# Three residual buffers, the next expert's copies ahead of the hidden product, filler products on TensorE, another group order, and the last x2 tile stored from ScalarE's queue

## What is computed

```python
x = x + token_mixer(rmsnorm(x), ...)          # its last product: merged @ w_out
x = x + hier_moe(rmsnorm(x), ...)
# hier_moe: 4 groups of 8 experts; top 1 group, then top 2 experts in it
lg = xt @ w_rg + b_rg; g_sel = top_k(softmax(lg), 1)
le = (xt @ w_re + b_re)[g_sel]; e_sel = top_k(softmax(le), 2)
h = silu(xb @ w1[e]) * (xb @ w3[e]);  y = (h @ w2[e]) * gate
```

## Time and profile before

| | us |
|---|---|
| median of 3 runs | 1255.5 |
| lowest, highest | 1253.0, 1255.56 |
| the profiled execution: its time | 1254.98 |
| its span, first to last instruction | 1253.3 |
| TensorE busy | 1114.9 (89% of the span) |
| VectorE, ScalarE, GpSimd busy | 510.9, 421.9, 229.9 |
| mean granted TensorE clock | 0.945 of full speed |
| read from and written to memory | 278.57 MB and 39.06 MB |

### The profile page before, as it was taken

The page is one execution under the profiler, slowest core; times in us unless marked ns, Lnnn a source line. Parts: engine busy times, 40 slices in busy tenths (PEclk is TensorE's granted clock), DMA queues, the critical chain, the costliest instruction groups (busy, mean ns, idle before and its releaser), DMA issues.

```text
span 1253.3 us, 15692 instructions
## 1 busy us (share of the span) xinstructions
PE 1114.9 (89%) x5136; PEld 684.8 (55%) x5136; DVE 510.9 (41%) x837; ACT 421.9 (34%) x658; POOL 229.9 (18%) x275
## 2 busy tenths in 40 slices
PE   5899999999988977999995699999999999898960
PEld 4688888888855645788784233333333333333320
DVE  5511111113237746755346244343515453424128
ACT  5322222223145655533114133333333342424222
POOL 0111101110007001000000033333323332423220
PEclk9899999999998967999996799999999999999985
DMA  8633331711160001746548989999999999999816
GB/s 320 233 118 118 112 114 50 284 47 45 50 252 2 1 1 42 246 133 241 195 158 331 420 340 375 419 420 419 421 419 365 421 420 420 420 420 420 336 36 276
DMA packets 69248, 308.89 MB, mean 246 GB/s; under 512 B 9025, under 2 KB 9153, under 8 KB 43873
## 3 DMA queue, kind: packets, MB, share of 16 engines
q1 hardware_dynamic: 56144, 273.86, 55.1%
q0 software_dynamic: 13072, 34.63, 7.2%
HBM read 278.57 MB, written 39.06 MB: 253 GB/s over the span
## 4 chain that ended last, share of the span: by engine, by line
PE 57%; DMA 22%; DVE 8%; ACT 6%; issue 5%; SPq 1%; DVEq 1%; ACTq 0%; POOLq 0%; POOL 0%
DMA rawe<-in_w 17%; PE ps L569 11%; PE ps L571 11%; PE ps L570 11%; PE ps L843 11%; PE ps L870 3%; ACT cur L1168 3%; PE ps L651 1%; DMA xres<-in_x_prompt 1%; PE ps L672 1%; PE ps L833 1%; DMA xrow<-in_x_sample 1%; DVE att L1316 1%; PE ps L684 1%; ACT prob L984 1%
## 5 line engine op out<-in xcount | busy, mean ns | idle before, releaser
L569 PE MATMUL ps<-whi,xTh 128*128 128x512 f32 x480 | 188.9, 394 | 18.5 <-DVE wlo L1199 14.0
L570 PE MATMUL ps<-wlo,xTh 128*128 128x512 f32 x480 | 188.5, 393 | 0.0
L571 PE MATMUL ps<-whi,xTl 128*128 128x512 f32 x480 | 188.2, 392 | 0.0
L843 PE MATMUL ps<-cur13a,xT 128*64 128x512 f32 x656 | 156.5, 619 | 25.9 <-DVEq L1601 25.1
L1199 DVE TENSOR_TENSOR wlo<-raw,whi 128x2048 fp32r<-128x2048 f32 x27 | 61.7, 2291 | 216.3 <-ACT whi L893 216.3
L843 PE MATMUL ps<-cur13b,xT 128*64 128x512 f32 x656 | 148.6, 592 | 0.0
L870 PE MATMUL ps<-cur,hT 128*64 128x512 f32 x640 | 146.2, 598 | 0.0
L1576 DVE COPY xT<-ps 128x512 f32<-128x512 f32 x41 | 28.3, 691 | 288.9 <-PE ps L833 288.9
L932 ACT ACTIVATE zst<-ps,rstd 128x512 f32<-128x512 f32 x60 | 41.3, 689 | 234.9 <-PE ps L571 232.8
L1168 ACT ACTIVATE cur<-rawe 128x4096 f32 x31 | 112.2, 3620 | 2.9 <-issue 0.2
L569 PEld LDWEIGHTS ps<-whi,xTh 128*128 128x128 f32 x480 | 91.1, 190 | 38.0 <-issue 18.8
(11 more groups left out here) (219 smaller groups left out, 1429.8 us busy)
## 6 DMA issues: line engine op xcount, KB each, us to landing
rawe<-in_w SPq DMA_DIRECT2D x96, 2048.0 KB
raw<-in_w_in SPq DMA_DIRECT2D x20, 1024.0 KB, 5.9
z_scratch<-zst POOLq DMA_DIRECT2D x60, 256.0 KB, 2.3
gat<-z_scratch SPq DMA_DIRECT2D x12, 512.0 KB, 3.7
xn_scratch<-rrow POOLq DMA_DIRECT2D x6, 1024.0 KB, 4.6
ya<-y_scratch SPq DMA_DIRECT2D x6, 1024.0 KB, 9.9
raw<-in_w_out SPq DMA_DIRECT2D x4, 1024.0 KB, 7.6
xcol<-in_x_cols SPq DMA_DIRECT2D x6, 512.0 KB, 10.2
```

The source lines that it names most:

```text
L569: pe.matmul(out, ah, bh, start=first, stop=False)
L570: pe.matmul(out, ah, bl, start=False, stop=False)
L571: return pe.matmul(out, al, bh, start=False, stop=last)
L843: mm = pe.matmul(ps[0][u * CAP:(u + 1) * CAP, :], xT[:, c, h * CAP:(h + 1) * CAP], cur13[h][:, :, c * 512 + u * 256:c * 512 + u * 256 + 25 ...
```

## The change

It joins six edits. (1) `xres` becomes three buffers with a semaphore each; the first three loads are queued ahead of expert 0, the others as soon as a buffer is free. (2) The store of the last x2 tile moves from SyncE to ScalarE, ahead of its squaring; SyncE queues expert 1 once the last w_out product is done and no longer after the last addition. (3) In `next_up` the copies of the next expert's w1 and w3 stand ahead of `xT` and `hh`; `cur13a` is released by a new semaphore at the middle of `up(b)`. (4) TensorE issues six products of 128x512 into `ps[7]`, which nothing reads, ahead of its wait for the number of blocks. (5) The groups are taken in the order 2, 0, 1, 3. (6) Router columns and ranks are laid out to match, on the host and in the constants.

```diff
+ORDER = (2, 0, 1, 3)
-    put("grank", NG - np.arange(NG))
+    put("grank", NG - np.array(ORDER))
-    xres = at("xres", F_O + 24 * KB, [P, D])
+    xres = [at(f"xres{s}", D_O + (20 + 4 * s) * KB, [P, D]) for s in range(3)]
...
-            for t in range(NT):
-                if t == 0:
-                    sp.wait_ge(s_mgd, 2 * NT)
-                else:
-                    sp.wait_ge(s_x2, 2 * t)
-                    x2_out(t - 1)
-                sp.dma_start(xres[:, :], x_tiles[t]).then_inc(s_xr, 16)
-                if t == 0:
-                    sp.wait_ge(s_lo, PRE)
-                    expert(0, 0)
-
-            sp.wait_ge(s_x2, 2 * NT)
-            x2_out(NT - 1)
+            for t in range(3):
+                residual(t)
+            sp.wait_ge(s_lo, PRE)
+            expert(0, EPG * ORDER[0])
+            for t in range(NT - 1):
+                sp.wait_ge(s_x2, 2 * t + 2)
+                x2_out(t)
+                if t < 3:
+                    residual(t + 3)
             sp.wait_ge(s_w, 2 * NT)
-            expert(1, 8)
+            expert(1, EPG * ORDER[1])
             sp.wait_ge(s_rr, NT)
             for p in range(2, 8):
-                expert(p, EPG * (p % NG) + p // NG)
+                expert(p, EPG * ORDER[p % NG] + p // NG)
...
+            def keep_busy(n):
+
+                for _ in range(n):
+                    pe.matmul(ps[7][:, :], ident, C("rel")[:, 0:512], start=True, stop=True)
+            keep_busy(6)
             pe.wait_ge(s_nb, 1)
...
-                mm.then_inc(s_13, 1)
+                    mm.then_inc((s_13a, s_13)[h], 1)
...
                 act.wait_ge(s_x2, 2 * t + 2)
+                if t == NT - 1:
+                    act.dma_start(x2_d[t * P:(t + 1) * P, :], x2[t % 3][:, :]).then_inc(s_x2s[t % 3], 16)
...
                 e, e1 = expert_of(dve, b), expert_of(dve, b + 1)
-                columns_of_rows(b + 1)
-                hidden(b)
                 with dve.If(e1 > e):
...
+                    dve.wait_ge(s_c13, 2 * e1)
                     for h in range(2):
+                        dve.wait_ge((s_13a, s_13)[h], b + 1)
                         dve.tensor_copy(cur13[h][:, :, :], pair[:, :, h * PIECE:(h + 1) * PIECE]).then_inc(s_c13, 1)
+                columns_of_rows(b + 1)
+                hidden(b)
```

More of the change, by code:

```diff
@@ L310, in hybrid_layer @@
         s_mTl = sem("s_mTl")
-        s_xr = sem("s_xr")
+        s_xr = [sem(f"s_xr{s}") for s in range(3)]
         s_w = sem("s_w")
@@ L348, in hybrid_layer @@
         s_13 = sem("s_13")
+        s_13a = sem("s_13a")
         s_sge = sem("s_sge")
@@ L528, in _, with residual @@
                 sp.sem_inc(k[2], 16)
-            for t in range(NT):
-                if t == 0:
-                    sp.wait_ge(s_mgd, 2 * NT)
-                else:
-                    sp.wait_ge(s_x2, 2 * t)
-                    x2_out(t - 1)
-                sp.dma_start(xres[:, :], x_tiles[t]).then_inc(s_xr, 16)
-                if t == 0:
-                    sp.wait_ge(s_lo, PRE)
-                    expert(0, 0)
-            sp.wait_ge(s_x2, 2 * NT)
-            x2_out(NT - 1)
+            def residual(t):
+                sp.dma_start(xres[t % 3][:, :], x_tiles[t]).then_inc(s_xr[t % 3], 16)
+            for t in range(3):
[7 more added lines that the diff above has]
+                    residual(t + 3)
             sp.wait_ge(s_w, 2 * NT)
-            expert(1, 8)
+            expert(1, EPG * ORDER[1])
             sp.wait_ge(s_rr, NT)
             for p in range(2, 8):
-                expert(p, EPG * (p % NG) + p // NG)
+                expert(p, EPG * ORDER[p % NG] + p // NG)
             with sp.Fori(0, 2) as i:
                 for q in range(12):
-                    expert(12 * i + (8 + q), 3 * i + (EPG * (q % NG) + 2 + q // NG), (8 + q) % RING)
+                    expert(12 * i + (8 + q), 3 * i + (EPG * ORDER[q % NG] + 2 + q // NG), (8 + q) % RING)
             sp.wait_ge(s_c13, 2 * NE - 4)
@@ L1491, in _ @@
                     choose(0, NT - 2)
-                dve.wait_ge(s_xr, 16 * (t + 1))
+                dve.wait_ge(s_xr[t % 3], 16 * (t // 3 + 1))
                 for n in range(2):
@@ L1498, in _ @@
                     dve.tensor_tensor(x2[t % 3][:, n * 512:(n + 1) * 512], ps[6 + n][:, :],
-                                      xres[:, n * 512:(n + 1) * 512], ALU.add).then_inc(s_x2, 1)
+                                      xres[t % 3][:, n * 512:(n + 1) * 512], ALU.add).then_inc(s_x2, 1)
                 dve.wait_ge(s_sq2, t + 1)
@@ L1761 @@
     laid["x_cols"] = _np.ascontiguousarray(x.transpose(0, 2, 3, 1).reshape(NT, P, D))
+    order = list(ORDER)
     laid["router_w"] = _np.ascontiguousarray(_np.concatenate(
-        [inputs["w_rg"][0][:, None, :], inputs["w_re"][0].transpose(1, 2, 0)], axis=1).reshape(D, NG + NE))
+        [inputs["w_rg"][0][:, None, order], inputs["w_re"][0][order].transpose(1, 2, 0)], axis=1).reshape(D, NG + NE))
     laid["router_b"] = _np.ascontiguousarray(_np.concatenate(
-        [inputs["b_rg"][0][None, :], inputs["b_re"][0].T], axis=0).reshape(NG + NE))
+        [inputs["b_rg"][0][None, order], inputs["b_re"][0][order].T], axis=0).reshape(NG + NE))
     for name in _INS + list(laid):
```

## The result

The changed kernel takes 1248.03 us (median of 5 runs, 1246.52 to 1248.8) against 1255.49 us (5 runs, 1253.0 to 1255.56). The ratio is 0.9944, with a 95% interval of 0.9931 to 0.9957: 7.5 us faster, where 9.5 were forecast. The profiled execution took 1247.31 us with a span of 1245.6, so its span is 7.7 us shorter.

The account below looks back on a forecast made before the run. It took the expert part as bound by TensorE and the weight stream close together, the end following the last waited-for landing. Earlier landing, latency and five blocks put the last `up` 9.5 us earlier: 1246 us, range 1240 to 1252.

Parts of the forecast that it names:

- Residual buffers: At the seam: TensorE's 2.17 us wait for `xres` and 1.7 us of half clock behind it go, -3.9 us.
- ScalarE's store: Last x2 store ahead of ScalarE's squaring: its issue costs 0.4 us (0.3 to 1); landing hidden up to 24 us.
- Expert 1 queued earlier: At the seam: starts the seam's 3.9 us and about 1 us more earlier, worth nothing by itself.
- Unread products: Ahead of the first `up`: last 4.2 to 5.2 us, may raise the clock; bounds 0 and -1.7, taken -0.5 us.
- First blocks and when the stream goes on: Place 0 has two blocks, place 1's `up` at 715.8, place 4's w2 issued at 731.9, 3.7 us later than before.
- So the 8.9 us of shortfalls go.: Weight stream in the expert loop: no more shortfalls, so from w2 issue to place 28's landing 387.8 us, landing at 1119.7.
- Latency of 7.0 and half clock behind it: At place 28: `up` comes 7.0 us after the weights land, and the clock's fall adds 1.7 us.
- Cadence, 11.72 and 0.2 for new experts: Last five blocks: 11.72 us each plus 0.2 for each of three new experts, 59.2 us.
- The sum: Last `up` at 1187.6 against 1197.15, -9.5 us, giving 1246; the sum sized differently had chance 0.68.
- The clock staying up: Rival: unread products give their whole 1.7 us and no clock fall follows place 28's wait; 1243, chance 0.13.
- Slower by a late store: Rival: last x2 store lands about 697 behind queued weights, `up(0)` some 12 us late; 1258, chance 0.08.

Follow-up runs that it names:

- e1: The kernel before with the three residual buffers alone; last `up` 3.2 us earlier counted from the seam's start, by the ratio 2 to 7 us.
- e8: The changed kernel with ScalarE's store of the last x2 tile issued behind its squaring; last `up` 2.7 us earlier counted from the seam's start.
- e10: The kernel before with residual buffers and group order, nothing else; ratio 0.9929 (0.9916 to 0.9942) against the kernel before.
- e4: The changed kernel with the w1 and w3 copies put back behind the hidden product; last `up` 1.7 us better counted from the seam's start.
- e2: The kernel before with group order 2, 0, 1, 3 alone; 4.4 us better counted from the seam's start, by the ratio 2 to 6 us.
- e9: The changed kernel with a wait ahead of queuing w1 of place 14, pausing the weight stream; ratio 0.9945 against the kernel before, median 1250.28 us.
- e5: The changed kernel with the groups in the old order 0, 1, 2, 3; ratio 0.9962 against the kernel before.
- e3: The kernel before with the early copies of w1 and w3 alone; ratio 0.9976 to 1.0013 against the kernel before.
- e6: The changed kernel without the six unread products; last `up` differed by 0.3 us counted from the seam's start.
- e7: The changed kernel with `cur13a` copied early and `cur13b` behind the hidden product; ratio 0.9900 to 0.9953 against the kernel before.
- e11: The changed kernel with split copies, no unread products and ScalarE's store behind its squaring; ratio 0.9910 (0.9891 to 0.9929) against the kernel before.

## Why the prediction was right, and where it was off

*Residual buffers, -3.9.* Right: 4.1 us at the seam, and e1 gave 3.2 at the end.

*ScalarE's store, +0.4.* Right to a tenth: the squaring began 0.40 us after the issue, and 0.4 us earlier from S in e8. The store landed after 9.1 us, far from the 24 that were free.

*Expert 1 queued earlier, 0.* Right by e10, which hasn't got it and loses nothing.

*Unread products, -0.5.* The bounds 0 and -1.7 both came: 0 in the changed kernel, -1.7 in e8 and e4. Their length was mis-sized, 7.4 us for 4.2 to 5.2. The rows from which I scaled it have the same shape, but float32r operands (`whi`, `mTh`): one such instruction started every 0.43 us at half clock. The unread products are float32, and their weight loads come every 0.85 us at half clock and every 0.43 at full.

*First blocks and when the stream goes on.* Place 1's `up` was forecast at 715.8, and the w2 issue at 731.9; they came at 715.24 and 731.36. Counted from S, `up(0)` came within 0.1 us of the forecast and the issue 0.5 later.

*"So the 8.9 us of shortfalls go."* They went, but the term was mis-sized. I took them off whole: 387.8 us from the issue to place 28's landing. It took 391.1. The 3.3 us between are what the shortfalls had been giving back: place 28 landed 7.0 us behind the count of its bytes, place 30 before only 3.3. This is the term that was most off: counted from S the last `up` was forecast 9.5 us earlier and came 6.6 earlier, 2.9 less. This term and a later issue are 3.3 and 0.5 us of that, and latency and cadence gave back 0.8.

*Latency of 7.0 and half clock behind it.* 6.7 us and 8.78 against 7.02 us: right. That the clock falls there is not sure of itself: it did in this execution and not in those of e2 and e10. *Cadence, 11.72 and 0.2 for new experts.* It was 11.72 without the 0.2: 0.6 us better.

*The sum.* -9.5 for the last `up`, measured -7.6 in the profiled executions, 1.0 of it from the mixer ahead of the seam, which the change does not touch: that much of the agreement is luck. By the medians it is -7.5. The range held the time.

*The rivals.* The clock staying up came half, in e8 and e4; in the changed kernel's own execution neither half came. "Slower by a late store" was far away. What I had not weighed as a rival is that the early copies come to nothing in sum: I had priced their 4.3 us at place 28, their saving on three blocks and the shortfalls that they help to remove, but never set the one against the others. e4 and e10 did.

## What to carry to other kernels

When compute and a stream of loads are nearly level, an edit is worth what it does to the last landing that is waited for and to the path behind it, not its saving times its count: 0.65 us at each of 31 changes of expert came to nothing, and moving heavy work ahead of that landing came to 4.4 us (2 to 6 by the ratio). A copy that waits for a landing should not stand in program order ahead of work that doesn't need it; splitting it kept the saving and gave 2.4 us of latency back. Before keeping a joined set, run its largest parts alone: here the residual buffers and the group order had all of the gain. And before a difference of 2 us between two profiled executions is put down to an edit, look whether the clock stayed up at the same places in both.

## What the runs showed of the hardware

- The 16 increments of one 2 MB load lay 2.7 us apart at place 9 and 11.4 at place 30 of a stream that ran unbroken at 420 GB/s, and 1.0 us behind a pause of 7.0 us. With that the lag between the bytes moved by count and the landing that VectorE saw grew from 3.7 us at place 18 to 7.0 at place 28. A shortfall of a stream that binds cost less than its length: 5.1 us for 7.0 (e9), 1.7 for 4.4 (e2, e4, e10).
- How long TensorE stood does not alone say whether the clock falls. In the block loop it fell to 1.2 GHz behind standing of 1.78 us (e9, at 869.8), 2.32 (e5), 2.33 (e3), 2.47, 2.66, 2.82 and most longer ones. It did not fall behind 1.71 and 1.84 (e10, e2), 2.33 and 2.34 (e6, e8), 2.40 (e7, e9, e11), nor once behind 3.77 (e1, at 1089.9, `up` 7.09 us). Where it fell behind the wait for place 28 or 30, `up` took 8.26 to 8.95 us, once 9.65, for 7.02.
- Twelve float32 instructions of 512 columns on a 128x128 weight tile took 7.4 and 7.6 us, 4.1 us of the 7.4 at 1.2 GHz. They did raise the clock. In six kernels it held until `up(0)` where TensorE stood 0.76 to 0.94 us behind them, and not where it stood 1.10 and 1.41.
